# Two norms behind the second network as one chain, and a new order of the S5 mixer's load queue

## The reference, cut to what matters

```python
def first_block(...):
    ...
    h = h + conv_ffn(rmsnorm(h, f_norm[1]), ...)      # the second network
    return rmsnorm(h, final_norm)                     # eps 1e-6: x of the second block

def second_block(x, c, ...):
    mod = silu(c) @ ada_w[i] + ada_b[i]
    sh1, sc1, g1, sh2, sc2, g2 = jnp.split(mod[:, None, :], 6, axis=-1)
    h = _rmsnorm(x, norm_mix_g[i]) * (1 + sc1) + sh1  # eps 1e-5
    y = _s5_mixer(h, ...)                             # i = 0
    x = x + g1 * y
    ...
```

## Time and profile before

| | us |
|---|---|
| median of 3 runs | 2811.62 |
| lowest, highest | 2808.92, 2815.66 |
| the profiled execution | 2810.29 |
| its span, first to last instruction | 2808.4 |
| mean granted TensorE clock | 0.969 of 2.4 GHz |

### The profile page before, as it was taken

The page is one execution under the profiler, slowest core; times in us unless marked ns, Lnnn a source line. Parts: engine busy times, 40 slices in busy tenths (PEclk is TensorE's granted clock), DMA queues, the critical chain, the costliest instruction groups (busy, mean ns, idle before and its releaser), DMA issues.

```text
span 2808.4 us, 36240 instructions
## 1 busy us (share of the span) xinstructions
PE 2682.6 (96%) x13867; PEld 2205.4 (79%) x13867; DVE 1523.0 (54%) x2025; ACT 1053.3 (38%) x1468; POOL 1206.7 (43%) x548
## 2 busy tenths in 40 slices
PE   7998799999999999999989999999999998999998
PEld 5877667888779667888877887888877887888887
DVE  4374457767686657646576556544554664322224
ACT  4543324343333653333333232232245673232322
POOL 3333333444444544444432135445434666444442
PEclk9899889999999999999989999999999999999999
DMA  4323113345324215555447436553323331223322
GB/s 131 105 76 89 46 45 107 118 142 157 114 93 140 76 46 158 177 175 182 140 135 235 133 117 227 182 192 106 102 71 115 108 103 61 90 90 98 97 91 74
DMA packets 365304, 333.14 MB, mean 119 GB/s; under 512 B 40752, under 2 KB 340208, under 8 KB 365040
## 3 DMA queue, kind: packets, MB, share of 16 engines
q1 hardware_dynamic: 331008, 264.03, 30.5%
q10 hardware_dynamic: 34160, 67.22, 6.8%
HBM read 308.56 MB, written 22.64 MB: 118 GB/s over the span
## 4 chain that ended last, share of the span: by engine, by line
PE 76%; DVE 6%; issue 2%; ACT 2%; POOL 1%; DMA 0%; ACTq 0%; SPq 0%; DVEq 0%; POOLq 0%
PE bank L269 20%; PE bank L271 20%; PE bank L270 20%; PE bank L283 2%; PE bank L284 2%; PE bank L288 2%; PE bank L1741 1%; PE bank L1750 1%; PE bank L1762 1%; PE bank L2436 1%; PE bank L2431 1%; DVE bank L444 1%; PE bank L369 1%; DVE sq_x L355 1%; PE bank L927 0%
## 5 line engine op out<-in xcount | busy, mean ns | idle before, releaser
L259 POOL TENSOR_TENSOR w_lo<-w_raw,w_hi 128x1024 fp32r<-128x1024 f32 x384 | 971.0, 2550 | 1297.4 <-ACT w_hi L207 1281.9
L269 PE MATMUL bank<-x_hi,w_hi 128*128 128x512 f32 x1936 | 764.7, 395 | 8.3 <-DVE y_val L1550 3.1
L270 PE MATMUL bank<-x_lo,w_hi 128*128 128x512 f32 x1936 | 757.6, 391 | 0.0
L271 PE MATMUL bank<-x_hi,w_lo 128*128 128x512 f32 x1936 | 757.3, 391 | 0.0
L207 ACT ACTIVATE w_hi<-w_raw 128x2048 fp32r<-128x2048 f32 x206 | 394.2, 1914 | 849.0 <-PE bank L271 761.1
L269 PEld LDWEIGHTS bank<-x_hi,w_hi 128*128 128x128 f32 x1936 | 366.2, 189 | 88.3 <-issue 8.8
L271 PEld LDWEIGHTS bank<-x_hi,w_lo 128*128 128x128 f32 x1936 | 365.9, 189 | 77.2
L270 PEld LDWEIGHTS bank<-x_lo,w_hi 128*128 128x128 f32 x1936 | 366.0, 189 | 77.1 <-issue 2.2
L269 PE MATMUL bank<-m_hi,w_hi 128*128 128x512 f32 x384 | 149.6, 390 | 0.0
L271 PE MATMUL bank<-m_hi,w_lo 128*128 128x512 f32 x384 | 149.4, 389 | 0.0
L270 PE MATMUL bank<-m_lo,w_hi 128*128 128x512 f32 x384 | 149.4, 389 | 0.0
(11 more groups left out here) (489 smaller groups left out, 4485.3 us busy)
## 6 DMA issues: line engine op xcount, KB each, us to landing
w_raw<-in_mlp_w SPq DMA_DIRECT2D x128, 512.0 KB, 4.5
ada_w<-in_ada_w ACTq DMA_DIRECT2D x96, 512.0 KB, 4.9
w_raw<-in_f_w_up SPq DMA_DIRECT2D x88, 512.0 KB, 5.1
w_raw<-in_m_w_in SPq DMA_DIRECT2D x40, 512.0 KB, 4.7
w_raw<-in_a_w_in SPq DMA_DIRECT2D x32, 512.0 KB, 4.9
w_raw<-in_f_w_down SPq DMA_DIRECT2D x32, 512.0 KB, 4.0
w_raw<-in_w_kv SPq DMA_DIRECT2D x16, 512.0 KB, 4.0
w_raw<-in_s_w_glu SPq DMA_DIRECT2D x16, 512.0 KB, 5.7
```

What stands on the lines that cost most here:

```text
L259: op = pool.tensor_tensor(w_lo[s][:, part], w_raw[s][:, part], w_hi[s][:, part].bitcast(F32), ALU.subtract)
L269: pe.matmul(dst, hi_l, hi_r, start=start, stop=False)
L270: pe.matmul(dst, hi_l, lo_r, start=False, stop=False)
L271: return pe.matmul(dst, lo_l, hi_r, start=False, stop=stop)
```

## The change

It has two parts. The first makes norms 4 and 5 from one pass over h. With a = the mean of h squared and b = the mean of (h * final_norm) squared, the scale of norm 5 over the raw h is 1 / sqrt(b + 1e-5 * a + 1e-5 * 1e-6) (`M_BOTH`), with the gain mix_gain * final_norm (`mid_gain`); the scale of norm 4 is 1 / sqrt(a + 1e-6) (`M_OWN`). During f1_dn2 ACT writes weighted squares (`weighted_act`, two per slot; in the last slot ahead of the weight split) and DVE adds them (`add_weighted`, six). `mid_pe` sums both kinds, five groups of four one-column matmuls; the spread of M_RBOTH goes to bank 5, that of M_ROWN to bank 4, then four keep-busy matmuls. The normed tiles lie in banks 6 and 7 instead of `xt`. h itself is scaled behind the normed tiles (`mid_scale_dve`); PE waits for that ahead of A0 and DVE ahead of the gate stage. Two small buffers of 96 and 32 bytes per partition are added ahead of the arena.

The second part moves entries of `s5_sp`: gate slots 2 and 3 go behind the returns of outputs 2 and 3, output 0's return goes ahead of chunk 7's matrix, and output matrices 5 behind it.

```diff
+        mid_col = sb("mid_col", [P, 6, TT])
+        mid_gain = sb("mid_gain", [P, KD])
...
+        MID_X = (bank[6][:, :], bank[7][:, :])
...
+        sqw, sqw_sum = at("sqw", 8, [P, 2, T]), at("sqw_sum", 12, [P, T])
+        def add_weighted(dve, k):
+            dve.wait_ge(w_sq, W_SQ + k + 1)
+            dve.wait_ge(mid_done, k + 1)
+            dve.tensor_tensor(sqw_sum[:, :], sqw_sum[:, :], sqw[:, k % 2, :], ALU.add).then_inc(mid_done, 1)
...
+                if c == 4 and 1 <= i * 2 + o < KD - 1:
+                    add_weighted(dve, i * 2 + o - 1)
...
+                    if f and c == 2 and i == 3:
+                        weighted_act(act, SLOTS["f1_dn2"], i)
                     split_hi(act, n + 2, i % 2, landed(n - i % 2 + 2))
...
+                        if c == 2 and i < 3:
+                            weighted_act(act, SLOTS["f1_dn2"], i)
...
+                if f and c == 2:
+                    dve.memset(sqw_sum[:, :], 0.0).then_inc(mid_done, 1)
...
-        def mid_dve(dve, c, c_next):
-            norm_root(dve, c)
-            squares_start(dve, c_next, SQ_B)
-            for k in range(KD):
-                dve.scalar_tensor_tensor(h[:, k, :], h[:, k, :], pcol("final_norm", k), RSTD, ALU.mult, ALU.mult).then_inc(mid_done, 1)
-                if k:
-                    add_square(dve, c_next, k - 1, (k - 1) % 2, SQ_B)
-        def mid_act(act, c_next):
-            for k in range(KD):
-                act.wait_ge(mid_done, k + 1)
-                act.wait_ge(n_acc, k + squared(c_next))
-                act.activation(sq[:, k % 2, :], h[:, k, :], ACT.Square).then_inc(n_sq, 1)
+        def weighted_act(act, base, i):
+            for k in (2 * i, 2 * i + 1):
+                act.wait_ge(bank_free, 2 * base + k + 1)
+                if k >= 2:
+                    act.wait_ge(mid_done, k)
+                act.activation(sqw[:, k % 2, :], h[:, k, :], ACT.Square, scale=pcol("final_norm", k)).then_inc(w_sq, 1)
+        def mid_pe(pe, c, sqs):
+            def sums(first, src, start, stop):
+                for j in range(TT):
+                    mm = pe.matmul(bank[4][:, first + j:first + j + 1], src[:, j * P:j * P + P], ones[:, 0:1],
+                                   start=(start and j == 0), stop=(stop and j == TT - 1))
+                return mm
+            pe.wait_ge(w_sq, W_SQ + KD - 1)
+            sums(TT, sqw[:, 0, :], True, False)
+            pe.wait_ge(n_acc, squared(c) + KD)
+            sums(0, sqs[1], False, False)
+            pe.wait_ge(mid_done, KD - 1)
+            sums(TT, sqw_sum, False, False)
+            pe.wait_ge(n_sq, KD * c)
+            sums(0, sqs[0][:, 1, :], False, False).then_inc(n_ss, 1)
+            pe.wait_ge(w_sq, W_SQ + KD)
+            sums(TT, sqw[:, 1, :], False, True).then_inc(n_ss, 1)
+            for n, dst, col in ((c, bank[5], M_RBOTH), (c + 1, ROWN, M_ROWN)):
+                pe.wait_ge(n_rcp, n + 1)
+                for j in range(TT):
+                    mm = pe.transpose(dst[:, j * P:j * P + P], mid_col[:, col, j:j + 1].to_broadcast([P, P]), ident[:, :])
+                mm.then_inc(n_bc, 1)
+            keep_busy(pe, bank[0], 4)
+        def mid_dve(dve, c):
...
+            dve.wait_ge(n_ss, c + 1)
+            dve.tensor_scalar(mid_col[:, M_EPS, :], bank[4][:, 0:TT], EPS2 / D, EPS2 * EPS1, ALU.mult, ALU.add).then_inc(mid_done, 1)
+            dve.wait_ge(mid_done, KD + 1)
+            dve.scalar_tensor_tensor(mid_col[:, M_BOTH, :], bank[4][:, TT:2 * TT], 1.0 / D, mid_col[:, M_EPS, :],
+                                     ALU.mult, ALU.add).then_inc(mid_done, 1)
+            dve.tensor_scalar(mid_col[:, M_OWN, :], bank[4][:, 0:TT], 1.0 / D, EPS1, ALU.mult, ALU.add).then_inc(mid_done, 1)
...
+        def mid_scale_dve(dve, c):
+            dve.wait_ge(n_bc, c + 2)
             for k in range(KD):
+                dve.scalar_tensor_tensor(h[:, k, :], h[:, k, :], pcol("final_norm", k), ROWN, ALU.mult, ALU.mult).then_inc(mid_done, 1)
...
             s_u_sp(sp, 7)
-            slot_glu(2)
             s_w_sp(sp, 5)
             s_v_sp(sp, 4)
-            slot_glu(3)
             s_w_sp(sp, 6)
-            s_v_sp(sp, 5)
             s_y_sp(sp, 0)
             s_w_sp(sp, 7)
+            s_v_sp(sp, 5)
             s_y_sp(sp, 1)
             s_v_sp(sp, 6)
             s_y_sp(sp, 2)
+            slot_glu(2)
             s_v_sp(sp, 7)
-            for j in range(3, 8):
+            s_y_sp(sp, 3)
+            slot_glu(3)
+            for j in range(4, 8):
                 s_y_sp(sp, j)
...
             slot_half(pe, 0, 0, x_hi, x_lo)
+            pe.wait_ge(mid_done, MID_SCALED)
             s_z_pe(pe, 0)
```

More of the change, by code:

```diff
@@ L337, in build, with lot_of @@
         NORM_X = (bank[2][:, :], bank[3][:, :])
+        MID_X = (bank[6][:, :], bank[7][:, :])
         SQ_X = (at("sq_x", 0, [P, 2, T]), at("sq_x_sum", 4, [P, T]))
         SQ_B = (sq, at("sq_sum", 36, [P, T]))
+        def lot_of(c):
+            return c if c < 5 else c - 1
         def squared(c):
-            return TT + KD * (c - 1)
+            return TT + KD * (lot_of(c) - 1)
         def squares_start(dve, c, sqs):
@@ L360, in add_square @@
         def add_square(dve, c, k, o, sqs):
-            dve.wait_ge(n_sq, k + (KD * c - KD + 1))
+            dve.wait_ge(n_sq, k + (KD * lot_of(c) - KD + 1))
             dve.wait_ge(n_acc, k + (squared(c) + 1))
@@ L384, in norm_sums_pe @@
                 keep_busy(pe, bank[5], 1)
-            pe.wait_ge(n_sq, KD * c)
+            pe.wait_ge(n_sq, KD * lot_of(c))
             for j in range(TT):
@@ L1301, in build @@
         o_n, o_g = sem("o_n"), sem("o_g")
+        w_sq, W_SQ = b_vc, 2 * TT
         def onorm_pe(pe):
@@ L1962, in b_out_dve @@
                 add_h(dve, BO, 2 + s, s, c, SQ_B)
-        mid_done = sem("mid_done")
-        def mid_dve(dve, c, c_next):
-            norm_root(dve, c)
-            squares_start(dve, c_next, SQ_B)
-            for k in range(KD):
-                dve.scalar_tensor_tensor(h[:, k, :], h[:, k, :], pcol("final_norm", k), RSTD, ALU.mult, ALU.mult).then_inc(mid_done, 1)
-                if k:
-                    add_square(dve, c_next, k - 1, (k - 1) % 2, SQ_B)
-        def mid_act(act, c_next):
-            for k in range(KD):
-                act.wait_ge(mid_done, k + 1)
-                act.wait_ge(n_acc, k + squared(c_next))
-                act.activation(sq[:, k % 2, :], h[:, k, :], ACT.Square).then_inc(n_sq, 1)
+        M_EPS, M_BOTH, M_OWN, M_RBOTH, M_ROWN = range(5)
@@ new lines, in build @@
+        ROWN = bank[4][:, :]
+        def weighted_act(act, base, i):
[12 more added lines that the diff above has]
+            sums(TT, sqw[:, 0, :], True, False)
+            pe.wait_ge(n_acc, squared(c) + KD)
+            sums(0, sqs[1], False, False)
[11 more added lines that the diff above has]
+            keep_busy(pe, bank[0], 4)
@@ new lines, in mid_dve @@
+        def mid_dve(dve, c):
+            dve.wait_ge(mod_done, 3)
+            dve.tensor_tensor(mid_gain[:, :], gain[:, 0, 0:KD], par[:, PAR["final_norm"]:PAR["final_norm"] + KD], ALU.mult).then_inc(mid_done, 1)
+            dve.wait_ge(n_ss, c + 1)
[4 more added lines that the diff above has]
+            dve.tensor_scalar(mid_col[:, M_OWN, :], bank[4][:, 0:TT], 1.0 / D, EPS1, ALU.mult, ALU.add).then_inc(mid_done, 1)
+            dve.wait_ge(n_std, c + 1)
+            dve.reciprocal(mid_col[:, M_RBOTH, :], mid_col[:, M_RBOTH, :]).then_inc(n_rcp, 1)
+            dve.wait_ge(n_std, c + 2)
+            dve.reciprocal(mid_col[:, M_ROWN, :], mid_col[:, M_ROWN, :]).then_inc(n_rcp, 1)
+            dve.wait_ge(n_bc, c + 1)
@@ new lines, in mid_act @@
+        def mid_act(act, c):
+            for n, src, dst in ((1, M_BOTH, M_RBOTH), (2, M_OWN, M_ROWN)):
+                act.wait_ge(mid_done, KD + 1 + n)
+                act.activation(mid_col[:, dst, :], mid_col[:, src, :], ACT.Sqrt).then_inc(n_std, 1)
+        def mid_scale_dve(dve, c):
+            dve.wait_ge(n_bc, c + 2)
+            for k in range(KD):
+                dve.scalar_tensor_tensor(h[:, k, :], h[:, k, :], pcol("final_norm", k), ROWN, ALU.mult, ALU.mult).then_inc(mid_done, 1)
@@ L1985, in build @@
+        MID_SCALED = 2 * KD + 3
         s5w = nc.dram_tensor("s5w", (S5Q, P, 1536), F32, kind="Internal").ap()
@@ L2634, in glu_dve @@
         def glu_dve(dve, c):
+            dve.wait_ge(mid_done, MID_SCALED)
             def gated(i, s):
@@ L3445, in _ @@
             ffn_act(act, 1, 5)
-            norm_act(act, 4, 0, split=False)
-            mid_act(act, 5)
-            norm_act(act, 5, 1, 5, shift=lambda k: mod[:, 0, k:k + 1], slot=SLOTS["s_in"])
+            mid_act(act, 4)
+            norm_hi(act, 5, SLOTS["s_in"], lambda k: mod[:, 0, k:k + 1], turned=MID_X)
             s5_act(act)
@@ L3482, in _ @@
             ffn_pe(pe, 1, 4)
-            norm_pe(pe, 4, SQ_X)
-            norm_pe(pe, 5, SQ_B)
+            mid_pe(pe, 4, SQ_X)
             s5_pe(pe, 5)
@@ L3519, in _ @@
             ffn_dve(dve, 1, 4)
```

(5 more changed lines are left out.)

2 lines of the change are left out of this document (1 added, 1 removed).

## The result

The changed kernel is slower: 2839.26 us (median of 4 runs, 2836.75 to 2840.85) against 2810.76 us for the kernel before on the same chip, ratio 1.0097, 95% interval 1.0084 to 1.0109. The forecast was 2788, in a range of 2781 to 2799. The profiled execution took 2840.56 us, its span is 2838.8.

What follows compares the result with a forecast made beforehand. PE, busy 96% of the span, was taken as the bound, so time is won only where it stands still or runs at low clock. 2810.3 - 7.8 (norms) - 14.9 (queue) = 2787.6, given as 2788, range 2781 to 2799.

Steps and rivals of the forecast that it cites:

- part 1: Norms 4 and 5 behind f1_dn2: one pass over h brings the projection earlier, net -7.8 us, ends -12 and -4.
- D: First turn of the S5 projection: the clock doesn't come back, +44 us less the gains, 2832 us; chance 0.03.
- The groups: Norm sums on PE: five groups of eight matmuls at 1.5 to 1.7 us each, ending at 1458.3.
- The adds meet POOL: DVE in f1_dn2: two adds meet the end of each POOL weight split; last square ends 3.2 us later.
- Part 2, the queue: SP queue of the S5 mixer: earlier matrix loads remove PE's wait and the half-clock work behind it, -14.9 us.
- the removed wait: PE ahead of S5 chunk 5: 5.66 us of waiting for its matrix shrink to 0.3, at worst 1.3.
- The size of the half-clock work: S5 products, outputs 2 and 3 and first gate part: 10.2 us saved if the clock holds.
- rival B: S5 matrix loads: chunk 5 or 6 waits 3.5 us or more, the clock goes too, 2800.5 us; chance 0.08.
- idle above 3 us: Sign that would prove the forecast wrong: PE idle for more than 3 us in either place watched.
- Rival A: S5 outputs: the clock falls though nothing waits, so the 10.2 us stay, 2797.8 us; chance 0.15.
- C: DVE adds in f1_dn2 are blocked: the norms gain only 2 to 4 us, 2792 us; chance 0.12.
- E: S5 chunk 5: the wait is for the POOL-delayed DVE chunk, so the queue edit does nothing, 2802.5 us; chance 0.04.

Runs made afterwards that it cites:

- the run with 256 bytes: The changed kernel with one more unused 128-byte buffer ahead of the arena, so activations lie 256 bytes higher than in the kernel before: 2795.24 us, ratio 0.9946.
- the mended kernel: The changed kernel with its two new buffers ahead of the weight buffers, so weights and activations move together: 2793.98 us, ratio 0.9937.
- the last kernel: Changed kernel with 256 added bytes, S5 matrix loads freed from table loads, output 3's gelu ahead of return 1's copy, return 1 ahead of table 7: 2784.7 us.

## Why the prediction was wrong

**The step that failed** is one sentence at the end of part 1: "The 128 bytes that move the arena: no row shows an effect of an address; nothing, ends ±1 us." It cost 44 to 46 us, and turned -16 into +28. That no row shows an effect was true, and was no bound: every row of the trace had been taken at one and the same distance. No row stands behind the ±1 us. A bound had to look at what the 128 bytes could reach, which is nearly every product: one per cent of PE's 2682.6 us is already 27 us. What the runs showed in its place: the large products start 232.5 ns apart instead of 226.7. The rival for slower, D, had another mechanism (a clock that doesn't come back) and did not occur: the clock is 1.00 in the changed kernel's windows from 1482.50, 2.3 us behind the first product, to 1545.

**Part 1, the norms** was right: -7.8 forecast, -8.6 measured in the run with the norms alone (-10.3 between the two marks). Inside it some terms differ, and some of them cancel. In the run with 256 bytes, where the products have their old pace:

```profile
1447.03 1.05 PE L2005 MATMUL bank<-ones,sqw 128*128 128x1 f32 x8 [1.22 <-ACT sqw L1999]
1447.94 1.03 PE L2005 MATMUL bank<-ones,sq_x_sum 128*128 128x1 f32 x8
1448.83 1.54 PE L2005 MATMUL bank<-ones,sqw_sum 128*128 128x1 f32 x8
1450.24 1.84 PE L2005 MATMUL bank<-ones,sq_x 128*128 128x1 f32 x8
1451.94 1.85 PE L2005 MATMUL bank<-ones,sqw 128*128 128x1 f32 x8
1454.69 1.97 PE L2021 MATMUL bank<-ident,mid_col 128*128 128x128 f32 x8 [0.90 <-DVE mid_col L2035]
```

The groups were priced at 1.5 to 1.7 each and took 6.8 us together from 1447.03, with the first two at full clock. (In the changed kernel all five were at full clock and took 4.7. From the last product to the projection it took 9.5 us, the kernels with the norms' part and the old pace 12.3 to 12.9.) The last product ends at 1445.8 here, so the sums are done 8.0 us behind it, where 9.7 was forecast. The adds meet POOL as forecast; here two of them in turn:

```profile
1439.43 2.86 DVE L372 TENSOR_TENSOR sq_x_sum<-sq_x_sum,sq_x 128x512 f32<-128x512 f32 x1
1442.21 2.88 DVE L464 TENSOR_TENSOR sqw_sum<-sqw_sum,sqw 128x512 f32<-128x512 f32 x1
```

and the last square of norm 4 begins at 1448.90, 3.1 us behind the end of the last product; before it was 0.8 (1449.37 against 1448.6). 2.3 us later, then, where 3.2 was forecast. From the last product to the projection it is 12.6 us instead of 23.5: 10.9 gained, more than the 8.8 of the prediction. In the run with the norms alone chunk 2 waits 1.88 us for the return of its u, where before it was chunk 3, for 0.86. That is not given back by the change: the run with the queue alone, with nothing edited up to there, shows 1.92 at chunk 2. Why the medians differ by 8.6 and the stretch by 10.3 is not accounted for; the place of the first mark alone scatters by more than that.

**Part 2, the queue** was half wrong: -14.9 forecast, -4.7 measured alone and -7.3 on top of the norms. Most of the removed wait was right: from 5.66 to 0 in the changed kernel and with the queue alone, but to 1.16 with 256 bytes and to 1.41 in the mended kernel, where 0.3, at worst 1.3, was forecast. The forecast took the DMA engines for half idle when chunk 5's matrix lands; with 256 bytes their share was 1.06 in the window from 1515.00. The size of the half-clock work was right. What failed is "Chunk 6's matrix waits for DVE's chunk 3 (ends 1531.0), lands 1535.5, wanted 1535.4: 0.1", and with it "Without the wait the clock should hold". PE waits 1.39 us there with both halves, 1.46 with the queue alone and 1.17 in the changed kernel, and each time the clock falls. In the mended kernel chunk 6 doesn't wait, and the clock falls in the 1.41 us ahead of chunk 5:

```profile
1517.19 1.98 PE L2483 MATMUL bank<-u,wring 128*64 128x64 f32 x32 [1.41 <-issue]
```

The dependence was named, but at a margin of 0.1 us against a landing that spreads over 2, and it was priced by its length alone. For rival B's "3.5 us or more" and for the "idle above 3 us" there was one row only, the long wait itself, in which the clock fell some 3.2 us after PE had stopped (0.67 in the window from 1532.50); no row between 0.86 and 5.66 us said what a shorter wait does. In the run with 256 bytes the clock was low from about 1524.2 to 1537.9: 13.6 us instead of 24, so of the forecast 10.2 us about half stayed lost; in the mended kernel it was low for 23.6 us, so nearly all.

**Rival A** (the clock falls there though nothing waits) is refuted by the last kernel, whose outputs and gate parts run at 1.00 from 1530 to 1560 with the same matmuls. **Rival B** (another load takes the place) is what happened, with a wait of a third of the length that it was given. **C** and **E** did not happen: the norms gained what was forecast, and chunk 5's wait was the matrix's. The mended kernel's 2793.98 lies inside the range of 2781 to 2799, but only as that range was held wide for A; the sum for part 2 was twice too large all the same.

## What to carry to other kernels

A new small buffer is a change to every access behind it. Before it is priced at nothing, compare the addresses mod 256 bytes of what TensorE loads and what it streams, and after it, compare the spacing of the products in a stage that the change doesn't touch; where that differs, the edit's own effect can't be read from the time. Put new small buffers where they move both operands or neither. And a wait of a little more than 1 us in a stretch of short matmuls is to be priced with what may follow it at half clock, while a load that serves two engines should be waited for, and issued, by each on its own.

## What the runs showed of the hardware that was not expected

- **The distance of the two operands of TensorE in SBUF.** With 128x512 float32r products back to back at 2.4 GHz, the spacing of their starts hangs on the distance from weights to activations mod 256 bytes: 226.7 ns at that of the kernel before, 228.9 at 64 bytes more, 232.4 at 128, 233.4 at 192 (the last two are 2.5 and 3% slower). It doesn't hang on either address alone. Only shifts of 0, 64, 128, 192 and 256 bytes were run. The Trainium skill (SBUF — State Buffer, A bandwidth-pool intuition that's wrong (but worth ruling out)) says that weight loads have a second, independent read port beside the moving operand; one would expect from it that their places don't matter to each other, and the runs (226.7 against 232.4 ns) disagree in that. How the two meet inside the memory no run here shows, nor whether products of another type are touched. The 256-column products that load activations and stream weights behave otherwise: 120.0 ns in the kernel before, 113.4 with 64 bytes, 118.7 to 120.0 with 128, 117.8 with 192.
- **How little idleness costs the clock among 64-column matmuls.** Waits of 1.17, 1.39, 1.41 and 1.46 us in the outputs went with a fall to 1.2 GHz, which came within the wait or 0.1 us behind it. One of 0.95 us did not, and neither did one of 1.16 us (ahead of chunk 5 with 256 bytes), so the length of the wait alone doesn't decide. Those of 1.51, 1.88 and 1.92 us ahead of chunk 2, which stand directly behind 512-column products, did not either; a wait of 2.60 us after one of 0.94 was followed by a fall. Once low, the clock stayed low for 10 to 24 us in which PE was busy, as in the 20.00 of 20 us of the earlier trace rows.
- **What a wait is put down to.** Three times the releaser named (the return `ych`, the matrices `tring`, "issue") was one that PE did not wait for or that had long been done; the queue and ACT's timeline gave the cause.
